# Four layers on one core: the features into a Second layer from the unnormalised residual

## What is computed

```python
def rms_norm_2(x, g):
    y = x * lax.rsqrt(jnp.mean(x * x, axis=-1, keepdims=True) + EPS_RMS)
    return y * g

x = rms_norm(x, norm_final)                   # the end of the First model
for l in range(DEPTH):                        # the Second model
    ...
    h = modulate(rms_norm_2(x, norm1_g[l]))   # a gain and a shift per column
    features = h @ w_in[l]                    # r, k, v, three lora parts, pool, gates
    ps = token_shift(features[shifted], mu)   # z + (previous token - z) * mu
    # tanh and sigmoid of the lora parts; wkv7 scan over r, k, v; multiscale_pool(pool)
    ...
    x = x + gate * (silu(h2 @ w_g) * (h2 @ w_u)) @ w_down[l]
```

## Time and profile before

| | us |
|---|---|
| median of 3 runs | 3521.26 |
| lowest, highest | 3519.79, 3522.5 |
| the profiled execution | 3527.62 |
| its span in the trace | 3525.5 |

### The profile page before, as it was taken

The page is one execution under the profiler, slowest core; times in us unless marked ns, Lnnn a source line. Parts: engine busy times, 40 slices in busy tenths (PEclk is TensorE's granted clock), DMA queues, the critical chain, the costliest instruction groups (busy, mean ns, idle before and its releaser), DMA issues.

```text
span 3525.5 us, 52850 instructions
## 1 busy us (share of the span) xinstructions
PE 3487.2 (99%) x21438; PEld 2856.0 (81%) x21438; DVE 2198.4 (62%) x3114; ACT 1342.0 (38%) x1576; POOL 0.2 (0%) x4
## 2 busy tenths in 40 slices
PE   8999999999999999999999999999999999999998
PEld 6788778888877887888888778988888778888887
DVE  6878667876288786687763656664233567673233
ACT  6565433322274644333222343233222443232223
POOL 0000000000000000000000000000000000000000
PEclk9999999999999999999999999999999999999999
DMA  4222224554232222345532341133222330133222
GB/s 126 87 72 72 76 94 159 176 193 139 87 98 87 72 72 72 120 144 190 191 120 87 94 131 38 50 120 107 95 96 86 94 131 27 62 129 98 95 96 72
DMA packets 275391, 366.57 MB, mean 104 GB/s; under 512 B 22668, under 2 KB 221056, under 8 KB 273920
## 3 DMA queue, kind: packets, MB, share of 16 engines
q1 hardware_dynamic: 249936, 313.44, 27.7%
q10 hardware_dynamic: 25264, 50.43, 4.1%
HBM read 353.89 MB, written 9.96 MB: 103 GB/s over the span
## 4 chain that ended last, share of the span: by engine, by line
PE 93%; DVE 3%; DVEq 1%; ACT 1%; issue 1%; DMA 0%; ACTq 0%; SPq 0%
PE banks L249 27%; PE banks L251 26%; PE banks L250 26%; PE banks L3315 1%; PE banks L3331 1%; PE banks L3259 1%; PE banks L3208 1%; PE banks L2216 1%; PE banks L2242 1%; PE banks L2259 1%; PE banks L1509 1%; PE banks L1522 1%; PE banks L588 0%; PE banks L617 0%; PE banks L618 0%
## 5 line engine op out<-in xcount | busy, mean ns | idle before, releaser
L249 PE MATMUL banks<-act_hi,w_hi 128*128 128x512 f32 x4064 | 1608.7, 396 | 5.5 <-ACT arena L1761 1.6
L251 PE MATMUL banks<-act_hi,w_lo 128*128 128x512 f32 x4064 | 1586.0, 390 | 0.0
L250 PE MATMUL banks<-act_lo,w_hi 128*128 128x512 f32 x4064 | 1584.9, 390 | 0.0
L171 DVE TENSOR_TENSOR w_lo<-w_raw,w_hi 128x2048 fp32r<-128x2048 f32 (+1 forms) x280 | 629.2, 2248 | 581.7 <-ACT w_hi L165 576.4
L249 PEld LDWEIGHTS banks<-act_hi,w_hi 128*128 128x128 f32 x4064 | 763.8, 188 | 198.0 <-issue 33.5
L251 PEld LDWEIGHTS banks<-act_hi,w_lo 128*128 128x128 f32 x4064 | 762.8, 188 | 161.9
L250 PEld LDWEIGHTS banks<-act_lo,w_hi 128*128 128x128 f32 x4064 | 763.5, 188 | 157.9 <-issue 3.8
L165 ACT ACTIVATE w_hi<-w_raw 128x2048 fp32r<-128x2048 f32 (+1 forms) x280 | 526.5, 1881 | 911.2 <-PE banks L251 862.8
L2426 DVE SCALAR_TENSOR_TENSOR arena<-arena,small 128x512 f32<-128x512 f32 x168 | 126.3, 752 | 13.2 <-issue 0.5
L249 PE MATMUL banks<-w_hi,act_hi 128*128 128x256 f32 x384 | 110.4, 287 | 0.4 <-DVE w_lo L171 0.4
L250 PE MATMUL banks<-w_lo,act_hi 128*128 128x256 f32 x384 | 108.8, 283 | 0.0
(11 more groups left out here) (427 smaller groups left out, 3395.5 us busy)
## 6 DMA issues: line engine op xcount, KB each, us to landing
w_raw<-in_w_in SPq DMA_DIRECT2D x98, 1024.0 KB, 5.4
arena<-in_ada_w ACTq DMA_DIRECT2D x24, 2048.0 KB, 8.0
w_raw<-in_ffn_up SPq DMA_DIRECT2D x48, 1024.0 KB, 5.4
w_raw<-in_w_gu SPq DMA_DIRECT2D x44, 1024.0 KB, 5.0
w_raw<-in_ffn_down SPq DMA_DIRECT2D x24, 1024.0 KB, 5.0
w_raw<-in_w_down SPq DMA_DIRECT2D x20, 1024.0 KB, 4.9
w_raw<-in_w_out SPq DMA_DIRECT2D x16, 1024.0 KB, 5.1
w_raw<-in_w_branch SPq DMA_DIRECT2D x12, 1024.0 KB, 5.0
```

What stands on the lines that cost most here:

```text
L171: self.core.nc.vector.tensor_tensor(view(self.lo[:, s]), view(self.raw[:, s]), view(self.hi[:, s]).bitcast(FP32), ALU.subtract)\
L249: nc.tensor.matmul(out, wh, ah, start=first, stop=False)
L250: nc.tensor.matmul(out, wh, al, start=False, stop=False)
L251: return nc.tensor.matmul(out, wl, ah, start=False, stop=last)
```

## The change

What it does, at both boundaries:

- **Lora on x times the gain.** `Outer.scaled` replaces `norm_twice` and the norm of `Second.back_scan`. While the adds of down run, ACT rounds x times the gain, and DVE takes the low part (L1172 of the changed kernel). The lora matmuls use these, in the order in which the adds come (`lora_pe`, banks 5, 7 and 3). Between them stand, after the sixth tile of slot 0, the column sums and the sums of squares, and after the eighth the spread. `turn_over` is gone from here.
- **Root and shift on the result.** DVE multiplies a lora bank by the root (`rooted`), ACT adds a column (`add_column`), and the token shift follows. The column is the shift times the weights: DVE forms it at the head of the stage (`shift_column`, eight operations for slot 0 and two for slot 1), PE sums it over partitions.
- **Pool on normalised tiles.** DVE and ACT form the normalised tiles after the spread, and `pe_next_normalised` follows them tile by tile.
- **Loads and splits.** Slot 0 of the lora weights is loaded in the stage before. The rkv0 weights of slot 0 are split ahead of `final_x` and the pool groups; those of slot 1 after group 3, as before. ACT's copy for group 0 goes ahead of tanh.
- At the first boundary `both_sums` forms 32 sums of two columns in one go, after all squares, and DVE adds up the eight tiles' shares.
- In `gate_up` the copy of the column out of PSUM becomes four small ones, and two semaphores become one.

```diff
+    def load_slot(self, sp, u, s, parts): ...
-    def scaled(self, gain, shift, root_wide, column_sums, column_at, shift_sums):
+    def scaled(self, gain, shift, root_wide, column_at, groups, before, twice=None):
...
+        def both_sums(pe):
+            columns(pe)
+            pe.wait_ge(n.squared, KD)
+            for i in range(KD):
+                for t in range(ST):
+                    at = 16 + 2 * (ST * i + t)
+                    ins = nc.tensor.matmul(ps[:, 4, at:at + 2], sq[i][:, t * P:t * P + P],
+                                           twice.sum_cols[:, self.order[i], :], start=True, stop=True)
+            ins.then_inc(n.summed, 1)
...
-            k.turn_over(pe, last_u, 0, 4)
...
+        between = {(0, 5): sums, (0, 7): spread}
+        if twice:
+            between = {(0, 5): both_sums, (0, 7): spread_both}
...
     # Second.inputs
+        def rooted(dve, b):
+            m = lora_rows[b]
+            dve.wait_ge(ring.done[b // 2], u_l + 1)
+            nc.vector.tensor_tensor(pad[b % 2][0:m, W:W + S], ps[0:m, lora_bank[b], :], root_wide[0:m, :], ALU.mult)\
+                .then_inc(n.normed, 1)
...
+            lora_pe(pe)
+            self.pe_next_normalised(pe, u["pool"], n, order)
             self.pe_feature(pe, u["rkv"])
...
     # its act_part
+            for at in range(5):
+                normalise_hi(act, at)
+            self.schedule.hi(act, u_l + 1, 1)
+            for at in range(5, KD):
+                normalise_hi(act, at)
             for b in range(3):
+                add_column(act, b)
+            self.schedule.hi(act, u["pool"] + 1, 0)
+            pool_step(act, 0)
             nc.scalar.activation(L0[0:64, :], L0[0:64, :], ACT.Tanh)
...
     # its dve_part
+            dve.wait_ge(n.root, 2)
+            normalised(dve, 0)
+            normalised(dve, 1)
+            self.schedule.lo(dve, u_l + 1, 0)
+            for at in range(KD):
+                lower(dve, at)
+                if at + 2 < KD:
+                    normalised(dve, at + 2)
+            self.schedule.lo(dve, u_l + 1, 1)
+            rooted(dve, 0)
+            rooted(dve, 1)
+            shift_dve(dve, 1, 0, self.col("mu_l0"), A[:, self.LORA, :])
+            dve.drain()
+            rooted(dve, 2)
+            dve.drain().then_inc(ring.bank_free[3], 1)
+            shift_dve(dve, 2, 1, self.col("mu_l1"), A[:, self.LORA + 1, :])
+            shift_dve(dve, 3, 0, self.col("mu_l2"), A[:, self.LORA + 2, :])
+            self.schedule.lo(dve, u["pool"] + 1, 0)
             if final_x is not None:
                 final_x(dve)
             for g in range(4):
                 pool_dve(dve, g)
-                if g % 2:
-                    self.schedule.lo(dve, u["pool"] + 1, g // 2)
+                if g == 3:
+                    self.schedule.lo(dve, u["pool"] + 1, 1)
...
+    def before_lora(self, down):
+        def part(dve):
+            dve.wait_ge(ring.loaded[0], u * 16 + 16)
+            self.shift_column(dve, ring.raw[:, 0].rearrange("p (k n) -> p k n", k=KD), total[:, 0:SLOT], self.shift1)
+            down.dve(dve)
+            dve.wait_ge(ring.loaded[1], u * 16 + 16)
...
+            nc.vector.tensor_tensor(scaled, ring.raw[:, 1].rearrange("p (k n) -> p k n", k=KD)[:, :, 0:64], ...)
+            dve.drain()
+            nc.vector.tensor_reduce(total[:, SLOT:SLOT + 64], scaled.rearrange("p k n -> p n k"), AX.X, ALU.add)
```

More of the change, by code:

```diff
@@ L125 @@
 PlainParts = namedtuple("PlainParts", "n gain order sums spread root_wide root_ok")
-ScaledParts = namedtuple("ScaledParts", "n gain shift order between root_wide root_ok column_at columns_ok")
+ScaledParts = namedtuple("ScaledParts", "n gain shift order between root_wide column_at")
 Conditions = namedtuple("Conditions", "load add sums")
@@ L152, in load, with load_slot @@
         for s in (0, 1):
[L153 to L156, removed]
+            self.load_slot(sp, u, s, parts[s])
+    def load_slot(self, sp, u, s, parts):
+        if not (isinstance(u, int) and u == 0):
+            sp.wait_ge(self.split[s], u)
+        for n, (dst, src) in enumerate(parts):
+            sp.dma_start(dst, src).then_inc(self.extra[s] if n else self.loaded[s], 16)
     def round(self, act, u, s, view, n_extra):
@@ L1131, in lo_of @@
                                                ALU.mult, ALU.subtract).then_inc(n.lo, 1)
[L1132 to L1135, removed]
+            before(dve)
             for i in range(KD):
@@ L1151, in scaled @@
[L1151 to L1178, removed]
-            k.turn_over(pe, last_u, 0, 4)
[L1180 to L1205, removed]
-            nc.vector.reciprocal(roots, roots).then_inc(n.rstd, 1)
-            k.normalise_dve(dve, n, nxt.gain1, nxt.shift1)
@@ L2666, in sp_part @@
             self.load(sp, ["up", "down"], more=False)
+            if isinstance(nxt, Second):
+                nxt.load_half(sp, "lora", 0)
         def pe_part(pe):
@@ L2812, in gate_tile, with inputs @@
         return self.arena[:, self.YB + q - 8 if q < 12 else self.K + q - 12, :]
-    def inputs(self, n, pool_w, lora_w, x_final, final_x=None):
+    def inputs(self, late, pool_w, lora_w, x_final, final_x=None):
+        n, gain, shift, order, between, root_wide, column_at = late
         nc, core, ring, ps, A = self.nc, self.core, self.ring, self.ps, self.arena
@@ new lines, in normalise_hi, with normalised @@
+        def normalise_hi(act, at):
+            act.wait_ge(n.normed, at + 1)
+            if at < KD - 1:
+                act.wait_ge(input_spent, at + 1)
+            else:
+                act.wait_ge(ring.done[1], u_l + 1)
+            nc.scalar.activation(self.hi[:, order[at], :], normed[at], ACT.Identity, bias=shift(order[at])).then_inc(n.hi, 1)
+        def normalised(dve, at):
+            m = order[at]
+            nc.vector.scalar_tensor_tensor(normed[at], self.x[:, m, :], gain(m), root_wide, ALU.mult, ALU.mult)\
+                .then_inc(n.normed, 1)
@@ L2936, in act_part @@
             act.drain().then_inc(act0, 1)
-            for g in range(4):
+            for g in range(1, 4):
                 pool_step(act, g)
@@ L3718, in gate_up @@
         u = self.u0["gu"]
-        n, gain, shift, order, between, root_wide, root_ok, column_at, columns_ok = late
+        n, gain, shift, order, between, root_wide, column_at = late
         silu_ok, used, spent = core.sem("silu_ok"), core.sem("silu_used"), core.sem("act_spent")
@@ L3939, in front @@
         out.x_ready = lambda dve: dve.wait_ge(x_in, 16)
-        n1, late = out.scaled(self.gain2, self.shift2, self.arena[:, 15, :], self.arena[:, 16, :], self.small[:, 4:8],
-                              self.shift_sums)
+        n1, late, _ = out.scaled(self.gain2, self.shift2, self.arena[:, 15, :], self.small[:, 4:8],
+                                 [self.arena[:, 16, j * P:j * P + P] for j in range(4)], self.before_up(out))
         def hidden(i, s):
```

210 lines of the change are left out of this document (137 added, 73 removed).

## The result

The changed kernel takes 3537.1 us, the median of five runs (3533.47 to 3539.61). Before it is 3521.26 over five runs. The ratio is 1.0044, with a 95% interval of 1.0032 to 1.0055: 15.8 us slower. The forecast was 3533.0, in a range of 3523 to 3541. The profiled execution took 3539.6 us, the longest of the five.

A forecast was written before the change was run, and what follows sets the result against it. TensorE, 99% busy, bounds the kernel now; after the change VectorE's chain from spread to rkv0's slot 1 split would hold it. +11.6 us at the first boundary and +0.1 at the second make +11.7: 3533.0 us, range 3523 to 3541.

The forecast's parts named there:

- Lora 15 us earlier, and nothing of it left: First boundary: lora starts 15.4 us earlier, at 1947.05, yet TensorE would reach rkv0's slot 1 at 2012.7, where it is now.
- VectorE's chain, 47.65 us: First boundary: VectorE's in-order work from its first normalised tile to the split of rkv0's slot 1 sums to 47.65 us.
- their lower bound of 0.65: VectorE's chain: each of three `rooted` operations priced at 0.73 us with hand-over, bounds 0.65 and 0.85.
- The row of sums at half clock: First boundary: 64 unbroken rows of sums take 11.6 us, the clock falling after 2.1 us; bounds 6.7 and 13.8.
- The wait ahead of slot 1, 9.6 and 6.4: TensorE stands idle ahead of rkv0's slot 1, 9.6 us at the first boundary and 6.4 at the second.
- The clock behind a stall, 2.2 each: After TensorE's stall at each boundary, a low clock costs 2.2 us, taken nearer the upper end because the stall is longer.
- the upper bound of 3.4: Clock after a stall: 3.4 us lost if the first 6.7 us after it run at half clock.
- The second boundary, +0.1: Second boundary: slot 1 of rkv0 starts 2.1 us earlier, the clock then costs 2.2, in sum +0.1 us.
- the forecast's main case: Whole kernel: VectorE's chain bounds, with the clock falling; between 3528.6 and 3537.6 us, chance 0.60.
- The clock didn't hold through the sums: Rival at the first boundary's sums: the clock holds, +4.1 us, 3525.3, or 3520.9 if stalls cost no clock; chance 0.15.
- VectorE didn't keep up: Rival at both boundaries: VectorE's chain fits into 38.1 us and TensorE bounds slot 1, -8.7 us, 3512.5; chance 0.08.
- Down's last split wasn't late: Rival at both boundaries: down's last split comes late behind the column, 3 us at each, +6, 3539; chance 0.15.

The follow-up runs named there:

- The second kernel: Changed kernel with the first boundary's 64 rows of two-column sums split into blocks of 8 or 16 between lora's first six tiles: 3533.3 us, ratio 1.0032.

## Why the prediction was right, point by point

- **Lora 15 us earlier, and nothing of it left.** Right. Lora starts with down's last matmul, and the first matmul of slot 1 is 8.7 us later than before, relative to it. What went ahead of the spread was cover for VectorE.
- **VectorE's chain, 47.65 us.** Right, on both boundaries within 0.2 us (49.35 and 45.4 from spread to slot 1, forecast 49.5 and 45.4). It could be summed that closely since all links but one have a row of before, and since in-order links on one engine add. The `rooted` operations, which had no row, took 0.64 each (1.28 for the first two), just under their lower bound of 0.65. The waits for ScalarE were taken at 1.5 together; its two roundings of weights cost VectorE 0.39 and 0.56.
- **The row of sums at half clock.** Right: 11.4 us (1952.54 to 1963.98) against 11.6, and the stretch from 1955.5 at 0.50 with TensorE busy 8.40 of 8.40. The second kernel shows the cause as far as it goes: the same 64 rows in blocks run at 1.00, in all three kept executions that have them. The rule of the Trainium skill (its page "TensorE: Matmul & The Clock Gate", section "Loop structure matters more than you think"), that matmuls back to back keep the clock up, doesn't cover this row: it stood back to back at either speed, and only what lay between its parts differed. Here the measurement decides.
- **The wait ahead of slot 1, 9.6 and 6.4.** A little too large, 8.3 and 4.9, as TensorE came later than I had it: it waits 0.44 us for a bank of rkv0 at the first boundary, and several slots took longer than 0.227 us a matmul. The first pool slot of the second boundary took 11.6 us in place of 10.9, and as long in the kernels where the clock didn't fall there. That changes how the delay is shared out, not slot 1's start.
- **The clock behind a stall, 2.2 each.** 2.4 and 3.0. The stretches at 0.50 behind the waits are some 5 and 6 us long, so the upper bound of 3.4 was sound. That the longer stall costs more, by which I chose 2.2, isn't borne out: over all runs a slot behind a wait of 4.9 us lost 1.7 to 3.0, behind one of 8.3 us 2.3 to 2.5.
- **The second boundary, +0.1: the step that was mis-sized.** The chain was right; the spread was not. I priced its last twelve matmuls at 2.7 us, at full clock, with a wait of 0.9 and eight narrow rows just ahead. Measured, the sums took 1.48 and the twelve matmuls 5.27 (2751.50 to 2756.77), at 0.52. Having let narrow rows bring the clock down at the first boundary, I should have put this one between 0 and 3 and widened the upper end. These 3.4, and 0.8 of clock behind the wait, are the 4.2 by which this boundary exceeds its sum in the profiled execution. The median exceeds the forecast by 4.1, but how much of that is this fall isn't shown, since it came in four of six executions only. That 3537.1 still lies under 3537.6, the upper bound of the forecast's main case, is in part luck: that bound was made of other terms (all sums at half clock, 3.4 lost at each stall), which came out lower.
- **The rivals.** The clock didn't hold through the sums. VectorE didn't keep up; its hand-overs and waits were as long as summed. Down's last split wasn't late: its input's low part ended at 1932.07 and TensorE started on that slot at about 1932.9, with no wait there; at the second boundary 2728.54 and 2729.16, the 0.6 us of the prediction. The column's second half waited 2.1 us for a load, and the first add there came 3.2 us after the start of down's last slot, where the estimate had 2.8.

## What to carry to other kernels

Moving matmuls ahead of a dependency also moves them off the engine that they covered: after such a change, sum the other engine's chain from the new dependency to the next thing TensorE needs, and look at which link stands last. Order inside a queue was worth more here than work saved: one split moved ahead of three pool groups that TensorE needs only later turned 16 us lost into 3 won, while leaving out 5.35 us of VectorE's work at one boundary gave 4.4. In these runs narrow matmuls were faster between wide ones than in a row.

## What the runs showed of the hardware

- The granted clock fell to 0.50 in a row of 64 two-column matmuls with TensorE busy throughout, and stayed at 1.00 with the same rows in blocks of 8 and 16 between wide ones. That held in five kept executions with the row and three with the blocks.
- It fell in four of six profiled executions around a wait of only 1.1 us with narrow rows on both sides, and in none of two without that wait, in which one group of the narrow rows stood elsewhere.
- A longer wait didn't cost more clock behind it: of the 48 matmuls that followed, 1.7 to 3.0 us behind five waits of 4.9, 1.8 behind one of 6.8, 2.3 to 2.5 behind three of 8.3, 3.0 behind one of 8.7.
